# Second gate panel and the output panels of the mixer as seven products in half contractions, with the weight quarters combined in place

## The chip, the cores and the metric

One Trainium2 chip, one of its cores. The metric is device microseconds (us) for one execution of the whole two-layer program. Three timed runs of the kernel before took 1997.31, 1997.37 and 1998.77 us, a median of 1997.37 us. All data are float32.

## The reference

Two decoder layers over 256 tokens of width 2048. A layer is a mixer (one input projection, whose columns go partly to sliding-window attention and partly to a gated delta rule, then one output projection) and a mixture of experts, each followed by a residual add and a LayerNorm.

```python
def hybrid_mixer(h, w_in, sinks, conv_w, a_log, dt_bias, dn_norm_w, w_out, cos, sin):
    proj = h @ w_in                                   # 256 x 2048 times 2048 x 5392
    sq, sk, sv, dn_qkv, dn_z, dn_a, dn_b = jnp.split(proj, cuts, axis=-1)
    ...
    attn_out = sliding_window_attention(sq, sk, sv, sinks)
    ...
    o = gated_delta_rule(dq, dk, dv, g, beta)
    o = (o * lax.rsqrt(jnp.mean(o * o, axis=-1, keepdims=True) + RMS_EPS)
         * dn_norm_w.astype(jnp.float32) * jax.nn.silu(z))
    return jnp.concatenate([attn_out, dn_out], axis=-1) @ w_out      # 2048 x 2048

for l in range(DEPTH):
    mix = hybrid_mixer(x, w_in[l], ...)
    x = layer_norm(ALPHA * x + mix, ln1_g[l], ln1_b[l])
    ffn = grouped_moe(x, router_w, router_bias, w_gate[l], w_up[l], w_down[l])
    x = layer_norm(ALPHA * x + ffn, ln2_g[l], ln2_b[l])
```

The change concerns the columns `dn_z` (the gate, 1024 columns, two panels of 512) of the input projection and the output projection `@ w_out` (2048 columns, four panels of 512).

## The kernel before, in words

**Panels and pieces.** The projections are worked off in panels of 512 output columns. A panel's weights come in four pieces of 512 rows (1 MB each), `j` = 0 to 3, in the order of the table `ORDER`, into a ring of four slots; TensorE frees a slot with `ring_free`, and SyncE issues the next load. Panels 0 to 10 are the input's (0: k and v; 1, 2: q; 3 to 8: delta-rule q, k, v; 9, 10: the gate z), 11 to 14 are the output's. A plain panel (`k_step`, L871; the last one in `last_panel`, L953) multiplies for each of its 16 blocks of 128 rows two token tiles of 128 by 512 columns: 32 matmuls.

**Seven products.** Panels in `FAST` (1, 2, 9, 13) use a Strassen-Winograd scheme: the two token tiles, pairs of row blocks and the two halves of the columns make a 2x2 block product that takes seven products instead of eight (`fast_unit`, L919; 28 units of two 256-column matmuls for a panel). It needs sums of the activations (`add_sums`), differences of the weight quarters (`combine`: four operations of 128x512 for each piece; VectorE for panels 1 and 2, GpSimd, here called POOL, for panels 9 and 13, L619 to L624) and the collection of the products out of four PSUM banks (`copy_first` on ScalarE, `collect` on VectorE, L1809 to L1816). Before, `combine` writes to spare buffers as soon as a piece has landed; only one of its results goes back into the ring.

**The delta rule.** After panel 9 the delta rule runs in two halves of four heads. In each, the 128x128 triangular systems of the chunks are inverted level by level (TensorE L1190, VectorE L2100, L2104, L2109), then the states and outputs follow, and `head_norm` (L2134 to L2140) normalises and gates them. TensorE works in program order; between the steps of the chain the code calls `meanwhile(n)`, which takes the next n matmul steps from a written-out list `left`: before, single k-steps of panels 10, 11 and 12. The last quarters of 11 and 12 come behind the chain, then fast panel 13, then plain panel 14. LayerNorm 1 (`layer_norm`, L2179 to L2186, VectorE) is done for token tile 0 while TensorE does tile 1 of panel 14.

**Experts.** SyncE then streams the weights of 16 experts, two at a time in 24 pieces of 1 MB, of which 16 have a place before the first pair starts (`first_home`, `first_pair`).

## Time and profile before

| | |
|---|---|
| median of three runs | 1997.37 us |
| the profiled execution | 1998.46 us, its span 1996.7 us |
| granted TensorE clock | 0.997 |
| TensorE busy | 1921.4 us (96% of the span) |
| VectorE busy | 686.5 us (34%) |
| ScalarE busy | 329.5 us (17%) |
| GpSimd busy | 103.0 us (5%) |
| HBM traffic | 535.73 MB read, mean 269 GB/s |

In the first layer the mixer takes from 0 to about 508 us, LayerNorm 1 and the router to 533 us, the experts to 985 us; the second layer repeats this. Busy shares are averages over these stages. A mark in brackets behind a row of a timeline says how long the engine sat idle before the row and what ended it. A float32 matmul is two instructions in the trace, so "x4" in a row of TensorE is two matmuls.

### The profile page before, as it was taken

To read this page: it belongs to the slowest core of one execution; us is meant where nothing else is said; L and a number is where in the kernel's file an instruction comes from. 1 tells how busy PE (TensorE), PEld (TensorE's weight loads), DVE (VectorE), ACT (ScalarE), POOL (GpSimd) and SP (SyncE) were. 2 spreads that over 40 slices of the span, in tenths; PEclk is the share of its full clock that TensorE was granted. 3 is DMA by queue.
4 is the path that set the end of the run, shared out by engine and by line. 5 is a ranking of instruction groups with operands and counts; after the bars stand their busy time and mean duration, and the time that the engine had idled before them with its cause. 6 is when DMAs were issued, how large, how long until landed. Compare 5 with 4: busy or idle time off the path is not lost.

```text
span 1996.7 us, 27957 instructions
## 1 busy us (share of the span) xinstructions
PE 1921.4 (96%) x11409; PEld 1194.3 (60%) x11409; DVE 686.5 (34%) x1385; ACT 329.5 (17%) x616; POOL 103.0 (5%) x174
## 2 busy tenths in 40 slices
PE   8999999999999999999899999999999999999996
PEld 7888886666644434444488888766665444443443
DVE  5444434553501111111483434445534011111104
ACT  1104220110311110111211231111103111110112
POOL 4000030012000000000000001200210000000000
PEclk9999999999999999999999999999999999999998
DMA  7433342228699999999934434422397999999995
GB/s 243 148 127 127 127 148 86 85 64 321 271 408 422 422 422 422 422 422 422 406 112 146 139 112 147 135 75 68 103 368 275 411 421 422 422 422 422 422 421 243
DMA packets 128842, 539.16 MB, mean 270 GB/s; under 512 B 15856, under 2 KB 20464, under 8 KB 78320
## 3 DMA queue, kind: packets, MB, share of 16 engines
q1 hardware_dynamic: 128752, 537.86, 69.0%
q8 instruction: 68, 1.11, 0.2%
q14 instruction: 22, 0.18, 0.0%
HBM read 535.73 MB, written 2.10 MB: 269 GB/s over the span
## 4 chain that ended last, share of the span: by engine, by line
PE 68%; DMA 25%; DVE 5%; issue 1%; ACT 0%; SPq 0%; DVEq 0%; ACTq 0%
PE bank L860 17%; DMA ring<-in_w_down_dram 13%; DMA ring<-in_w_up_dram 12%; PE bank L1405 10%; PE bank L871 9%; PE bank L919 8%; PE bank L1453 6%; PE bank L1190 3%; PE bank L953 3%; PE bank L1337 3%; PE bank L787 1%; DMA x_t<-in_w_up_dram 1%; PE bank L1066 1%; PE bank L1349 0%; PE bank L1161 0%
## 5 line engine op out<-in xcount | busy, mean ns | idle before, releaser
L860 PE MATMUL bank<-x_t,ring 128*128 128x256 f32 x1536 | 342.6, 382 | 0.0
L860 PEld LDWEIGHTS bank<-x_t,ring 128*128 128x128 f32 x1536 | 288.4, 190 | 48.8 <-issue 11.2
L2333 DVE TENSOR_TENSOR region_a<-bank,region_a 128x512 f32<-128x512 f32 x16 | 11.1, 692 | 566.3 <-PE bank L1405 566.3
L1405 PE MATMUL bank<-ring,region_a 128*64 128x512 f32 x704 | 159.6, 596 | 13.1 <-DMA ring<-in_w_up_dram 13.1
L1337 PEld LDWEIGHTS bank<-prob_t,x_nat 128*128 128x128 f32 x1024 | 115.5, 192 | 12.0 <-issue 11.4
L871 PE MATMUL bank<-ring,mix_acc 128*128 128x512 f32 x256 | 121.3, 604 | 1.4 <-ACT mix_acc L1663 1.4
L1453 PE MATMUL bank<-ring,region_a 128*64 128x512 f32 x512 | 115.1, 594 | 5.9 <-DMA ring<-in_w_down_dram 5.8
L1337 PE MATMUL bank<-prob_t,x_nat 128*128 128x128 f32 x1024 | 118.6, 277 | 0.0
L1405 PEld LDWEIGHTS bank<-ring,region_a 128*64 128x64 f32 x704 | 51.6, 137 | 109.3 <-issue 107.6
L1453 PE MATMUL bank<-region_b,region_a 128*64 128x512 f32 x384 | 113.3, 596 | 1.7 <-ACT region_a L1710 1.7
L2346 DVE SCALAR_TENSOR_TENSOR y_lo<-bank,slot_gate,y_hi 128x512 fp32r<-128x512 f32 x64 | 48.0, 750 | 193.1 <-ACT y_hi L1722 187.9
L919 PE MATMUL bank<-ring,x_t 128*128 128x256 f32 x416 | 100.7, 380 | 0.0
L1405 PE MATMUL bank<-region_b,prob_t 128*64 128x512 f32 x336 | 98.4, 592 | 0.0
L619 POOL TENSOR_TENSOR ring<-ring 128x512 f32<-128x512 f32 x16 | 20.3, 1271 | 1350.7 <-DMA ring<-in_w_in_dram 1002.2
L1453 PEld LDWEIGHTS bank<-ring,region_a 128*64 128x64 f32 x512 | 38.0, 137 | 80.3 <-issue 80.3
L919 PEld LDWEIGHTS bank<-ring,x_t 128*128 128x128 f32 x416 | 78.2, 190 | 12.7 <-POOL ring L622 1.5
L1405 PE MATMUL bank<-ring,prob_t 128*64 128x512 f32 x288 | 65.0, 595 | 13.2 <-DMA ring<-in_w_up_dram 13.2
L1190 PEld LDWEIGHTS bank<-region_a 64*64 64x64 f32 x1920 | 59.1, 135 | 30.3 <-issue 30.3
L1453 PEld LDWEIGHTS bank<-region_b,region_a 128*64 128x64 f32 x384 | 34.5, 137 | 71.1 <-issue 57.1
L2328 DVE TENSOR_TENSOR mix_acc<-bank,mix_acc 128x512 f32<-128x512 f32 x120 | 73.3, 680 | 7.9 <-PE bank L1351 7.8
L1722 ACT ACTIVATE y_hi<-bank,slot_gate 128x512 fp32r<-128x512 f32 x64 | 44.0, 687 | 190.4 <-PE bank L1453 190.4
L919 PE MATMUL bank<-ring,mix_acc 128*128 128x256 f32 x288 | 69.7, 380 | 0.6 <-DVE ring L1846 0.6
(424 smaller groups left out, 2413.0 us busy)
## 6 DMA issues: line engine op xcount, KB each, us to landing
ring<-in_w_up_dram SPq DMA_DIRECT2D x88, 1024.0 KB, 19.5
ring<-in_w_in_dram SPq DMA_DIRECT2D x80, 1024.0 KB, 5.0
ring<-in_w_down_dram SPq DMA_DIRECT2D x64, 1024.0 KB, 23.4
region_b<-in_w_gate_dram SPq DMA_DIRECT2D x48, 1024.0 KB, 19.6
region_b<-in_w_down_dram SPq DMA_DIRECT2D x48, 1024.0 KB, 20.6
ring<-in_w_gate_dram SPq DMA_DIRECT2D x36, 1024.0 KB, 22.4
ring<-in_w_out_dram SPq DMA_DIRECT2D x32, 1024.0 KB, 5.2
x_t<-in_w_up_dram SPq DMA_DIRECT2D x32, 1024.0 KB, 19.1
```

Source lines behind the costliest of these rows:

```text
L619: pool.tensor_tensor(t1, b12, b11, ALU.subtract).then_inc(combined_ready.sem, 1)
L860: m = pe.matmul(b[c // 2][:, (c % 2) * T:(c % 2 + 1) * T], w[:, kk, c * P:(c + 1) * P], xT[:, k, :], start=(k == 0 and c % 2 == 0), stop=( ...
L871: m = pe.matmul(b[t][:, 0:width], lhs[:, k, t * P:(t + 1) * P], w[:, k if kind == "kv" else kk, 0:width], start=(k == 0), stop=(k == KC - 1))
L919: mm = pe.matmul(o, lhs[:, a, :], rhs[:, a, :], start=(j == a == 0 and name in FIRST_IN_BANK), stop=(j == 3 and a == 1), skip_group_check= ...
L953: m = pe.matmul(bank[PAIR_OF_BANKS[i][t]][:, :], mixT[:, k, t * P:(t + 1) * P], piece(n)[:, kk, :], start=(k == 0), stop=(k == KC - 1))
L1190: m = pe.matmul(out_of(t, h)[rows, :], lhs_of(t, h, rows), rhs_of(t, h, rows), start=True, stop=True)
L1337: m = pe.matmul(bank[GATHER_BANKS[b]][:, j * P:(j + 1) * P], x_nat[:, t, c * P:(c + 1) * P], pick2[:, t, :], start=(t == 0), stop=(t == NT ...
L1405: m = pe.matmul(bank[2 + w][rows, :], xg_half[k // 8][:, k % 8 * P + rows.start:k % 8 * P + rows.stop], weights(n + e)[:, kk * PANEL:(kk + ...
L1453: m = pe.matmul(bank[4 + c][rows, :], hid_t[:, f, rows], weights(n + e)[:, c * PANEL:(c + 1) * PANEL], start=(f == 0), stop=(f == FC - 1))
L1722: act.activation(y_hi[:, c * PANEL:(c + 1) * PANEL], bank[4 + c][:, :], ACT.Copy, scale=slot_gate[:, 0:1]).then_inc(hi_ready.sem, 1)
L2328: tt(a, bank[SCATTER_BANKS[n]][:, :], a, ALU.add).then_inc(scat_added.sem, 1)
L2346: stt(out=y_lo[:, cols], in0=bank[4 + c][:, :], scalar=slot_gate[:, 0:1], in1=y_hi[:, cols], op0=ALU.mult, op1=ALU.subtract).then_inc(y_re ...
```

## The change

The second gate panel (10) and the output panels become products of seven as well. The output panels are cut into half contractions: the front half (rows 0 to 1023, the attention part, pieces `j` = 0, 1) of all four, and the back half (pieces 2, 3) of panels 11, 12 and 13. Each half panel has its own seven products over 14 units, is collected by VectorE and added to the residual `x_nat` (`add_half`). Only the back half of panel 14 stays plain. The order of the pieces follows: front halves of 11 to 14, then back halves.

`combine` now works in place on the ring: each quarter is overwritten once the products that need it as loaded (P1, P2, P3) have run, which the semaphore `raw_done` tells. POOL combines panels 9, 10, the four front halves and the back half of 11; VectorE combines panels 1 and 2, and the back halves of 12 and 13. Units are reordered: the as-loaded products of piece n+1 come ahead of the combined ones of piece n.

In VectorE's program the collections stand at chosen places in the delta rule (`between`, and at the start and end of a half). Panel 8 is done one token side after the other. The early loads of six expert pieces stand together behind the last piece of `w_out`, and two more wait for `spare_free`.

```diff
-    FAST = [1, 2, 9, 13]
+    FAST = [(1, (0, 1, 2, 3)), (2, (0, 1, 2, 3)), (9, (0, 1, 2, 3)), (10, (0, 1, 2, 3))]
+    FAST += [(i, (0, 1)) for i in range(N_IN, N_IN + 4)]
+    FAST += [(i, (2, 3)) for i in range(N_IN, N_IN + 3)]
+    GATE0, GATE1, FRONT, BACK = 2, 3, 4, 8
-    PRODUCTS = [("P1", 0, 0), ("P2", 1, 0), ("P6", 1, 1), ("P5", 2, 0), ("P7", 2, 1), ("P4", 3, 1), ("P3", 3, 0)]
+    AS_LOADED, COMBINED = ("P1", "P2", "P3"), ("P5", "P7", "P6", "P4")
@@ POOL and VectorE, combine(): the same on both @@
-                pool.wait_ge(mix_landed[n % RING].sem, ...)
-                pool.tensor_tensor(t1, b12, b11, ALU.subtract).then_inc(combined_ready.sem, 1)
-                pool.tensor_tensor(t2, b22, t1, ALU.subtract).then_inc(combined_ready.sem, 1)
-                pool.tensor_tensor(b12, b22, b12, ALU.subtract).then_inc(combined_ready.sem, 1)
-                pool.tensor_tensor(t4, b21, t2, ALU.subtract).then_inc(combined_ready.sem, 1)
+                pool.wait_ge(raw_done.sem, raw_done.at(l, 2 * m + 1))
+                pool.tensor_tensor(b11, b12, b11, ALU.subtract).then_inc(combined_ready.sem, 1)
+                pool.wait_ge(combined_ready.sem, combined_ready.at(l, 4 * m + 1))
+                pool.tensor_tensor(b12, b22, b12, ALU.subtract).then_inc(combined_ready.sem, 1)
+                pool.wait_ge(combined_ready.sem, combined_ready.at(l, 4 * m + 2))
+                pool.wait_ge(raw_done.sem, raw_done.at(l, 2 * m + 2))
+                pool.tensor_tensor(b22, b22, b11, ALU.subtract).then_inc(combined_ready.sem, 1)
+                pool.wait_ge(combined_ready.sem, combined_ready.at(l, 4 * m + 3))
+                pool.tensor_tensor(b21, b21, b22, ALU.subtract).then_inc(combined_ready.sem, 1)
...
-                for f in range(2, N_FAST):
-                    for j in range(4):
+                for f in range(GATE0, BACK + 1):
+                    for j in FAST[f][1]:
                         combine(l, f, j)
@@ TensorE @@
+                def units_of(f):
+                    pieces = FAST[f][1]
+                    loaded = [[(f, j, name) for name in AS_LOADED] for j in pieces]
+                    mixed = [[(f, j, name) for name in COMBINED] for j in pieces]
+                    if f == BACK:
+                        return loaded[0] + mixed[0] + loaded[1] + mixed[1]
+                    units = loaded[0]
+                    for n in range(1, len(pieces)):
+                        units = units + loaded[n] + mixed[n - 1]
+                    return units + mixed[-1]
...
-                left = [(10, k, t) for k in range(KC) for t in range(NT)]
-                left += [(i, k, t) for i in (11, 12) for k in range(8) for t in range(NT)]
-                left += [(i, k, t) for i in (11, 12) for k in range(8, 12) for t in range(NT)]
+                left = [unit for f in range(GATE1, BACK) for unit in units_of(f)] + units_of(BACK)[:7]
...
-                fast_panel(13)
+                meanwhile(len(left))
+                fast_panel(BACK, 7)
+                fast_panel(BACK + 1)
+                fast_panel(BACK + 2)
                 last_panel()
@@ VectorE @@
-                combine(0, 3)
+                for j in range(1, 4):
+                    combine(0, j)
...
-                combine(1, 0)
+                def between(half, lev):
+                    if (half, lev) == (0, 2):
+                        dve.wait_ge(pv_read.sem, pv_read.at(l, n_q // 2))
+                        add_sums(mixT, front_sums, 0, 4)
+                    if (half, lev) == (0, 4):
+                        collect_second_sixth(GATE1)
+                        collect_fifth_seventh(GATE1)
+                    if (half, lev) == (0, 5):
+                        collect_third_fourth(GATE1)
+                    if (half, lev) == (1, 1):
+                        collect_third_fourth(FRONT + 1)
+                    if (half, lev) == (1, 2):
+                        add_half(FRONT + 1)
+                    if (half, lev) == (1, 4):
+                        add_sums(mixT, back_sums, 4, 6, 4)
...
                         dve.wait_ge(o1_done.sem, o1_done.at(l, 1))
+                        collect(FRONT)
+                        add_half(FRONT)
...
+                for f in range(BACK, N_FAST):
+                    collect(f)
+                    add_half(f)
+                    if f < N_FAST - 1:
+                        for j in FAST[f + 1][1]:
+                            combine(f + 1, j)
```

How the order changes, at three places. First VectorE at the start of the second layer: the last pieces of panel 1 are combined (`ring<-ring`, four rows a piece), x is rescaled (`x_nat<-x_nat,region_cd`), panel 1 is collected and rotated. Before:

```order
L1889 COPY v_nat<-bank 128x128
L1844 TENSOR_TENSOR ring<-ring 128x512
L1846 TENSOR_TENSOR ring<-ring 128x512
L1847 TENSOR_TENSOR ring<-ring 128x2x256
L1849 TENSOR_TENSOR ring<-ring 128x512
L1899 TENSOR_TENSOR x_nat<-x_nat,region_cd 128x2048 x2
L1902 TENSOR_TENSOR x_nat<-x_nat,region_cd 128x2048 x2
L1844 TENSOR_TENSOR ring<-ring 128x512
L1846 TENSOR_TENSOR ring<-ring 128x512
L1847 TENSOR_TENSOR ring<-ring 128x2x256
L1849 TENSOR_TENSOR ring<-ring 128x512
L1809 TENSOR_TENSOR region_cd<-bank,first_product 128x2x256
```

The same place now, from the last piece of panel 1 on:

```order
L1874 TENSOR_TENSOR ring<-ring 128x2x256
L1876 TENSOR_TENSOR ring<-ring 128x2x256
L1879 TENSOR_TENSOR ring<-ring 128x2x256
L1881 TENSOR_TENSOR ring<-ring 128x2x256
L1930 TENSOR_TENSOR x_nat<-x_nat,region_cd 128x2048 x2
L1933 TENSOR_TENSOR x_nat<-x_nat,region_cd 128x2048 x2
L1816 TENSOR_TENSOR region_cd<-bank,first_product 128x2x256
L1825 TENSOR_TENSOR region_cd<-bank,region_cd 128x2x256
L1826 TENSOR_TENSOR region_cd<-bank,region_cd 128x256
L1833 TENSOR_TENSOR region_cd<-bank,region_cd 128x2x256
L1860 TENSOR_TENSOR v_rot<-region_cd,cos_t 128x512
```

The first piece of panel 2 was combined ahead of panel 1's collection; it now comes behind collection and rotation, and the last piece of panel 1 waits for its own as-loaded products.

Second, VectorE at the start of the second half of the delta rule, from the last two operations of `head_norm` of the first half. Before:

```order
L2138 TENSOR_TENSOR region_cd<-region_cd,rms 128x512
L2140 TENSOR_TENSOR region_cd<-region_cd 128x512
L2055 TENSOR_SCALAR region_a<-bank,gc 128x128 x4
L2065 TENSOR_TENSOR region_a<-bank,region_a 128x512
L2069 TENSOR_TENSOR region_a<-bank,region_a 128x256 x2
```

And now, the same stretch:

```order
L2195 TENSOR_TENSOR region_cd<-region_cd,rms 128x512
L2197 TENSOR_TENSOR region_cd<-region_cd 128x512
L1816 TENSOR_TENSOR ring<-bank,first_product 128x2x256
L1825 TENSOR_TENSOR ring<-bank,ring 128x512
L1826 TENSOR_TENSOR ring<-bank,ring 128x256
L1833 TENSOR_TENSOR ring<-bank,ring 128x512
L1849 SCALAR_TENSOR_TENSOR x_nat<-x_nat,ring 128x2x512
L2104 TENSOR_SCALAR region_a<-bank,gc 128x128 x4
```

Five operations (collection and residual add of the first front half) now stand ahead of the decay's four.

Third, TensorE behind the chain of the second half: L787 (now L793) transposes the gated outputs. Before:

```order
L871 MATMUL bank<-ring,mix_acc 128x512 x2
L787 MATMUL bank<-ident,region_cd 128x128 x4
L871 MATMUL bank<-ring,mix_acc 128x512 x11
L787 MATMUL bank<-ident,region_cd 128x128 x4
L871 MATMUL bank<-ring,mix_acc 128x512 x9
```

And now (the sources of the products are the ring and, in turn, `mix_acc` and its sums in `ring` and `x_t`):

```order
L928 MATMUL bank<-ring,mix_acc 128x256 x2
L928 MATMUL bank<-ring 128x256 x2
L793 MATMUL bank<-ident,region_cd 128x128 x4
L928 MATMUL bank<-ring 128x256 x6
L928 MATMUL bank<-ring,mix_acc 128x256 x2
L928 MATMUL bank<-ring 128x256 x6
L928 MATMUL bank<-ring,mix_acc 128x256 x6
L928 MATMUL bank<-ring,x_t 128x256 x6
L793 MATMUL bank<-ident,region_cd 128x128 x4
L928 MATMUL bank<-ring,x_t 128x256 x2
```

Eleven plain steps between the two transposes became 13 units (26 matmuls of 256 columns).

## Rows read from the trace of the kernel before

**Rows 1.** Busy time by stage (windows); columns as in the first line.
```profile
core 0: us, PE busy (x) PEld busy (x) DVE busy (x) ACT busy (x) POOL busy (x), PEclk, DMA share, GB/s
297.00:508.00 211.00, 209.81 (x1764) 133.55 (x1763) 101.39 (x202) 19.56 (x32) 21.08 (x16) 1.00 0.41 148
...
585.00:640.00 55.00, 55.00 (x288) 24.98 (x286) 8.97 (x15) 9.29 (x16) 0.00 (x0) 1.00 1.01 417
640.00:985.00 345.00, 322.24 (x1630) 144.44 (x1627) 53.27 (x90) 46.04 (x80) 0.00 (x0) 1.00 1.01 421
```

**Rows 2.** The chain that ended last: start us, us, what.
```profile
300.85 4.29 PE bank L871 x10
...
456.64 24.17 PE bank L919 x112
480.81 27.48 PE bank L953 x64
...
510.07 2.35 DVE region_a L2179
```

**Rows 3.** Timeline of VectorE, layer norm of tile 0, start of tile 1.
```profile
494.58 0.69 DVE L2165 SCALAR_TENSOR_TENSOR x_nat<-x_nat,bank 128x512 f32<-128x512 f32 x1 [10.32 <-PE bank L953]
...
498.80 3.92 DVE L2186 SCALAR_TENSOR_TENSOR x_nat<-region_a,ln_s 128x512 f32<-128x512 f32 x4
```

**Rows 4.** Timeline of POOL, combining without and with company.
```profile
437.13 1.26 POOL L622 TENSOR_TENSOR ring<-ring 128x512 f32<-128x512 f32 x1
438.36 1.71 POOL L624 TENSOR_TENSOR ring<-ring 128x512 f32<-128x512 f32 x1
```

**Rows 5.** Timeline of VectorE, a level, the second half's start, its end.
```profile
328.32 0.76 DVE L2104 TENSOR_TENSOR region_a<-bank,region_a 128x256 f32<-128x256 f32 x2 [2.31 <-PE bank L1190]
...
372.93 1.13 DVE L2055 TENSOR_SCALAR region_a<-bank,gc 128x128 f32<-128x128 f32 x4 [2.78 <-PE bank L1161]
...
376.94 0.69 DVE L2071 TENSOR_TENSOR region_a<-bank,region_a 128x512 f32<-128x512 f32 x1
...
393.59 0.42 DVE L2096 TENSOR_TENSOR region_a<-region_a,ident_c 128x256 f32<-128x256 f32 x1
...
436.68 0.69 DVE L2149 TENSOR_TENSOR region_cd<-bank,region_cd 128x512 f32<-128x512 f32 x1
437.40 1.54 DVE L2134 TENSOR_TENSOR region_a<-region_cd 128x512 f32<-128x512 f32 x1
```

**Rows 6.** Timeline of TensorE, where it would wait for those.
```profile
378.06 1.04 PE L787 MATMUL bank<-ident,region_b 128*128 128x128 f32 x8
...
394.56 1.15 PE L1190 MATMUL bank<-region_a 64*64 64x64 f32 x32
...
437.42 0.66 PE L787 MATMUL bank<-ident,region_cd 128*128 128x128 f32 x4
...
448.64 7.99 PE L871 MATMUL bank<-ring,mix_acc 128*128 128x512 f32 x18 [0.69 <-ACT mix_acc L1663]
```

**Rows 7.** Timeline of VectorE, second layer: rescaling of x, panel 1.
```profile
1027.87 4.49 DVE L1899 TENSOR_TENSOR x_nat<-x_nat,region_cd 128x2048 f32<-128x2048 f32 x2
1032.39 4.49 DVE L1902 TENSOR_TENSOR x_nat<-x_nat,region_cd 128x2048 f32<-128x2048 f32 x2
...
1039.46 0.68 DVE L1809 TENSOR_TENSOR region_cd<-bank,first_product 128x512 f32<-128x512 f32 x1
...
1046.52 0.69 DVE L1844 TENSOR_TENSOR ring<-ring 128x512 f32<-128x512 f32 x1 [0.22 <-DVE region_cd L1914]
```

**Rows 8.** Timeline of TensorE, second layer: panel 1, decay inputs, panel 2.
```profile
1012.87 1.89 PE L919 MATMUL bank<-ring,x_t 128*128 128x256 f32 x8
...
1037.57 1.93 PE L984 MATMUL bank<-x_t,prob_t 128*32 128x256 f32 x32
...
1048.08 1.97 PE L919 MATMUL bank<-ring,mix_acc 128*128 128x256 f32 x8 [0.60 <-DVE ring L1846]
```

**Rows 9.** Timeline of VectorE beside POOL's second operation (435.57 to 437.17).
```profile
435.96 0.68 DVE L2147 TENSOR_TENSOR region_cd<-bank,gfac 128x512 f32<-128x512 f32 x1
```

More of the change, by code:

```diff
@@ L175, in trunk @@
         spare = ring[:, RING:RING + 2, :].rearrange("p r n -> p (r n)")
-        def combined(m, which):
-            at = (m % 2) * 6 * HW + which * 2 * HW
-            return spare[:, at:at + 2 * HW].rearrange("p (a n) -> p a n", a=2)
         mix_acc = sb("mix_acc", [P, KC * T])
@@ L877, in k_step @@
-                    if tiles[-1] == 0:
-                        return
-                    if k == KC - 1:
-                        m.then_inc(proj_done.sem, 1)
-                        owed[0] += kind != "kv"
-                    elif kk == 3 and kind != "kv":
-                        m.then_inc(ring_free.sem, 1)
-                def fast_unit(i, j, name):
-                    f = FAST.index(i)
-                    m, n = 4 * f + j, ORDER.index((i, j))
-                    src, added, sums = (xT, 2, x_sums) if i < N_IN else (mixT, 4, mix_sums)
-                    s1, s2, s3, s4 = (v[:, 2 * j:2 * j + 2, :] for v in sums)
-                    t1, t2, t4 = (combined(m, which) for which in range(3))
+                            m = pe.matmul(b[t][:, 0:2 * kv_dim], xT[:, k, t * P:(t + 1) * P], kv_w[:, k, :],
+                                          start=(k == 0), stop=(k == KC - 1))
@@ L913, in fast_unit @@
-                    if name in ("P6", "P5", "P7", "P4"):
-                        seen = {"P6": 2, "P5": 2, "P7": 3, "P4": 4}[name]
-                        pe.wait_ge(combined_ready.sem, combined_ready.at(l, 4 * m + seen))
-                    _, at, half = next(x for x in PRODUCTS if x[0] == name)
-                    o = bank[FAST_BANKS[i][at]][:, half * HW:(half + 1) * HW]
+                        if i >= N_IN and j < 2:
+                            pe.wait_ge(pv_read.sem, pv_read.at(l, n_q // 2))
+                        elif i >= N_IN:
+                            pe.wait_ge(to_read.sem, to_read.at(l, j))
@@ L1101, in _ @@
                     .then_inc(gc_done.sem, 1)
-                panel(8)
+                for side in range(2):
+                    for k in range(KC):
+                        k_step(8, k, (side,))
                 pe.wait_ge(rows_ready.sem, rows_ready.at(l, 1))
@@ L1234, in _ @@
                     meanwhile(1)
-                    assert not left or left[0][0] > 10
                     pe.wait_ge(inv_ready.sem, inv_ready.at(l, (half + 1) * LEVELS))
@@ L1817, in collect, with add_half @@
                     dve.wait_ge(fast_read.sem, fast_read.at(l, 3 * f + 3))
+                def collect(f):
+                    collect_second_sixth(f)
+                    collect_fifth_seventh(f)
+                    collect_third_fourth(f)
+                def add_half(f):
+                    i = FAST[f][0] - N_IN
+                    xs = x_nat[:, :, i * PANEL:(i + 1) * PANEL]
+                    held, at = half_panel(f)
+                    mixed = held[:, at:at + NT * PANEL].rearrange("p (t n) -> p t n", t=NT)
+                    if f < BACK:
+                        s.do(stt(out=xs, in0=xs, scalar=ALPHA, in1=mixed, op0=ALU.mult, op1=ALU.add))
+                    else:
+                        s.do(tt(xs, xs, mixed, ALU.add))
@@ L1917, in _ @@
                     if i == 0:
-                        for j in range(1, 4):
+                        for j in range(4):
                             combine(1, j)
@@ L2101, in _ @@
                         m.then_inc(masked_ready.sem, 1)
+                        between(half, lev)
                         dve.wait_ge(tlt_done.sem, tlt_done.at(l, n_tlt + lev))
@@ L2121, in _ @@
                     m.then_inc(inv_ready.sem, 1)
+                    if half:
+                        collect(FRONT + 2)
+                        add_half(FRONT + 2)
                     if half == 0:
```

351 lines of the change are left out of this document (171 added, 180 removed).

## The prediction, made before the changed kernel was run

> **What bounds the kernel now.** I read the windows by stage first. In the mixer's second part (297 to 508 us) TensorE is busy 209.8 of 211 us at full granted clock, the DMA engines 41% of it, VectorE half of it [rows 1]. Among the experts the picture turns: at 585 to 640 us TensorE is full and the DMA at 417 GB/s, from 640 us to 985 us the DMA runs at 421 GB/s and TensorE idles 23 us. So the experts end a fixed time after they start, whatever the mixer does, provided that the 16 pieces with early homes have landed; what the mixer saves or loses shows in full, once for each of the two layers. The chain of waits agrees: in the mixer it is TensorE's matmuls almost without a break [rows 2], until LayerNorm 1 on VectorE.
>
> **TensorE's own work.** A plain step is 4.29/5 = 0.858 us, a plain panel 27.48 us, a fast panel 24.17 us, so a unit 24.17/28 = 0.863 us [rows 2]. From behind panel 9 to the end of the projections there were three plain panels in steps (3 x 27.46), one fast and one plain: 134.0 us. Now there are 28 + 7 x 14 = 126 units and 16 plain matmuls: 108.8 + 13.7 = 122.5 us. Saved: 11.5 us a layer, 23.0 us in all. Nothing else that TensorE does changes. The rest is what VectorE, POOL and their waits give back.
>
> **Half-hidden work in the delta rule.** TensorE takes one unit between the steps, as before, and works in order. So each late VectorE result stalls it.
> - Level 2 of half 0: `add_sums`, four 512-wide operations of 0.69 us and their gaps, 2.85 us, into an idle stretch of 2.31 us [rows 5]. It delays the inverse by 0.6 us. The pieces of the collections at levels 4, 5, 1 and 2 are 0.7 to 1.9 us and fit there.
> - Start of half 1: collecting (0.69 + 0.69 + 0.42 + 0.69 and gaps, 2.6 us) and `add_half` (1024 wide, 1.3 us) stand ahead of the decay, into 2.78 us of idle time; 1.1 us late. TensorE has 0.43 us to spare there (376.94 + 0.69 = 377.63 against 378.06) [rows 5, 6]. 0.7 us.
> - Start of the inverse, half 1: 0.73 us more against 394.56 - 394.01 = 0.55 us [rows 5, 6]. 0.2 us.
> - Each fast group needs its banks emptied. I went through the units one by one: the second-sixth, fifth-seventh and third-fourth collections stand in VectorE's order before the units that overwrite those banks are reached, so no further wait, 0.
>
> **Combining on POOL, behind the products.** POOL needs four operations of 1.26 us and 0.08 us gaps [rows 4], 5.3 us from the end of P1; the last, P4, is reached five units after P1, 4.3 us. In the delta rule units are spread out and this is hidden. In the back half of panel 11 they are dense and the pieces not interleaved: 1.0 us for each of two pieces, the transposes between give 0.5 us back, 1.5 us. For panels 12 and 13 VectorE combines after it has collected the group before: 0.7 + 1.3 us, then four times 0.72, 4.9 us from the end of the last P4, where TensorE has six as-loaded units, 5.2 us. No wait, by 0.3 us.
>
> **Contention of VectorE and POOL.** VectorE's operations with both inputs in SBUF grow where they meet a POOL operation: 1.54 us instead of 0.69 at 437.40, which ends 0.55 us behind POOL's (437.13 + 1.26), and POOL's next takes 1.71 instead of 1.26 [rows 4, 5]. So a meeting costs VectorE about 0.85 us. Before, POOL worked 21 us in this stretch (16 operations) [rows 1]; now, panel 9 left out, 56 operations, 71 us. Where VectorE's path is the one TensorE waits for:
> - the outputs of half 1: `head_norm` of tile 0 must be over for `o_ready`, which came at 437.37 against TensorE's 437.42 [rows 5, 6]. Two more of its operations now meet POOL: 1.5 us (both ends: 0 to 2.5);
> - masks and inverses at the start of both halves' levels, the decay's mask in half 1: 0.5 + 0.8 + 0.4 us (0 to 4);
> - POOL itself delayed in the back half of 11 by `add_half` and `add_sums`: 0.5 us (0 to 1.5).
> Together 3.7 us a layer; 0 if the phases miss, 8 if all meet.
> The Trainium skill (SBUF — State Buffer, Who interferes with whom) says that such an operation and a GpSimd instruction that reads SBUF exclude each other for a whole instruction, so the loser waits for the rest of the other's. On average that would be half of POOL's 1.26 us, 0.63 us a meeting in place of the row's 0.85, and 2.7 us in place of 3.7.
>
> **LayerNorm 1.** Tile 0 takes from 494.58 to 502.72, 8.1 us [rows 3]. It was hidden behind 13.7 us of tile 1; now tile 1 of the last half panel is 6.9 us. Tile 1's norm starts 1.3 us behind its matmuls. An old wait of 0.69 us before the last quarters [rows 6] goes.
>
> **Head of layer 2.** The last piece of panel 1 is now combined after its P3, 20 units in: 1012.87 + 17.3 = 1030.1, two dependent operations end at 1031.6. The rescaling (9.1 us) thus starts 3.8 us later than at 1027.87 [rows 7, 8], the collection ends its first row at 1041.4, and what took 7.1 us from 1039.46 to 1046.52 brings the first combination of panel 2 to 1047.6 and its result to 1048.3. TensorE has only six as-loaded units behind 1039.5: it is ready at 1044.7 and waits 3.6 us in all, where it waited 0.6 [rows 8]. 3.0 us, once; layer 1 has no rescaling and ends its rotation 3 us ahead of need.
>
> **Loads.** A ring slot is held from P1 to P4, and refilled with 12 us in hand. The eight expert pieces now go out together when TensorE is through with panel 12, some 26 us before the end of the projections instead of 28 to 40. Eleven pieces at 2.5 us (1 MB at 421 GB/s [rows 1]) are 27 us, and the first pair starts 25 us behind the projections' end. Hidden with over 10 us in hand: 0.
>
> **The sum.** A layer: -11.5 + (0.6 + 0.7 + 0.2) + 1.5 + 3.7 + 1.3 - 0.7 = -4.2. Twice that and 3.0 is -5.4 us, from the profiled execution's 1998.46: 1993.1. That execution stands 1.1 us above the median of the runs, so against the median 1992.0.
>
> **Rivals.**
> - *Clean overlap.* Phases miss, POOL and VectorE hardly meet: the 3.7 us go. -12.7 us, 1984.7. For it: rows where VectorE reads a bank while POOL works show no growth (0.68 us at 435.96 inside 435.57 to 437.17 [rows 9]), and most of the chain is of that kind. Against: `o_ready` has 0.05 us to spare.
> - *Everything meets.* Contention of 7 us a layer, or another tight place that I take as covered (VectorE's 0.3 us for panels 12 and 13) opens. +1.3 us or somewhat less, 1995 to 2000: no change. For it: POOL's share rises from 21 to over 70 us in that stretch.
> - *Slower: the level loop itself slows.* If VectorE's operations with one input in a PSUM bank also wait while POOL reads SBUF, each of some six levels a layer beside POOL loses two waits of 0.85 us. The path there has only about 0.2 us to spare, so 10 us a layer: 1993 + 20 - 1, about 2012 with all, 2003 with half. It decides from 2.1 us more a layer than in my sum. Against it stands the single pair of rows [rows 9], seen while POOL ran, and for it only that before no level ever ran beside POOL. The same page of the Trainium skill has it that an operation with at most one SBUF input does not contend; by that this rival is worth nothing.
> - *TensorE isn't shortened.* The units would have to run at 0.95 us instead of 0.863, and the 11.5 us a layer would be gone: 2015. The rate of such units is in the trace [rows 2], so I give it no chance of its own.
>
> **Chances.** Forecast 0.45, 1988 to 1995.5; clean overlap 0.22; everything meets 0.23; slower 0.10. What a measurement tells from no change is 0.2%, 4 us. Below 1993.4 lie most of the first and all of the second: faster 0.56. Same: the rest of the first and the third, 0.33. Slower 0.11. The range is 1983 to 2000, from clean overlap with POOL's waits halved to everything meeting; the forecast's own is 1988 to 1995.5.
>
> **What would show it.** TensorE's busy time falls by 20 us or more, and its idle time in each mixer grows by some 7 us, in the second half of the delta rule and at the back half of panel 11, ended by VectorE and POOL. Operations with two SBUF inputs in `head_norm` have a mean of 1 us or more, the level loop's stay at 0.38 us each. A gap of about 2 us ended by VectorE before the combined products of panel 2, in the second layer alone. LayerNorm of tile 1 starts 1 to 1.5 us late. The experts take as long as before. If the level loop slows, if collections leave TensorE idle at the front halves, or if the first pair waits for a load, the prediction is wrong.

## The result, and the profile after

The changed kernel takes 2003.21 us (median of 17 runs, 1999.87 to 2005.69), the kernel before, timed beside it, 1998.76 us (17 runs, 1997.07 to 2000.66). The ratio is 1.0023, 95% interval 1.0016 to 1.0031: slower by some 4.5 us. Forecast were 1992.0 and a range of 1983 to 2000. The profiled execution has a span of 2001.8 us, 5.1 us longer than before.

The first lines of the page of the changed kernel:

```profile
span 2001.8 us, 28926 instructions
...
PE 1907.0 (95%) x11745; PEld 1257.9 (63%) x11745; DVE 772.1 (39%) x1483; ACT 333.7 (17%) x630; POOL 213.5 (11%) x254
```

The windows by stage, with the columns of [rows 1]:

```profile
297.00:508.00 211.00, 201.99 (x1934) 166.28 (x1933) 141.30 (x252) 21.76 (x39) 76.42 (x56) 0.99 0.38 133
585.00:640.00 55.00, 55.00 (x293) 25.66 (x292) 8.97 (x15) 8.40 (x15) 0.00 (x0) 1.00 1.01 419
640.00:985.00 345.00, 321.57 (x1627) 143.85 (x1627) 51.27 (x87) 45.20 (x78) 0.00 (x0) 1.00 1.01 422
```

The experts are as they were. In the mixer's second part TensorE is busy 7.8 us less than in [rows 1], and the stretch is no shorter: the time turned into waits. These are its waits in that part of layer 1 (waiting line, the line waited for, us in total, times, longest):

```profile
PE bank L1187 <- DVE region_a L2147: 3.8, 2, 2.3
PE bank L793 <- DVE region_cd L2206: 1.5, 1, 1.5
PE bank L793 <- DVE region_a L2120: 1.4, 1, 1.4
PE bank L928 <- POOL ring L628: 1.2, 2, 1.0
PE bank L928 <- POOL ring L633: 0.4, 2, 0.2
PE bank L928 <- POOL ring L631: 0.2, 1, 0.2
PE bank L1228 <- DVE region_a L2170: 0.2, 1, 0.2
```

That is ten waits; before, there were two, of 0.7 and 0.2 us. L1187 is the inverse's product at level 1, L793 the transposes of k (behind L2120) and of the outputs (behind L2206), L928 a product of a fast panel, L1228 the last level of an inverse.

The largest group lies at level 1 of the second half. The timeline of VectorE, POOL and TensorE there (start us, us, engine, line, operation):

```profile
398.00 1.27 POOL L626 TENSOR_TENSOR ring<-ring 128x512 f32<-128x512 f32 x1 [8.93 <-PE bank L928]
398.09 1.45 DVE L2146 TENSOR_TENSOR region_a<-region_a,ident_c 128x256 f32<-128x256 f32 x1
399.35 1.32 POOL L628 TENSOR_TENSOR ring<-ring 128x512 f32<-128x512 f32 x1
399.47 1.48 DVE L2147 TENSOR_TENSOR region_a<-region_a,ident_c 128x256 f32<-128x256 f32 x1
...
401.09 1.74 PE L1187 MATMUL bank<-region_a 64*64 64x64 f32 x32 [2.31 <-DVE region_a L2147]
402.76 2.07 PE L928 MATMUL bank<-ring 128*128 128x256 f32 x4
```

An operation that took 0.42 us [rows 5] takes 1.45 and 1.48. Each of the two ends just behind a POOL operation: 398.09 + 1.45 = 399.54 behind 399.27, 400.95 behind 400.67. These two rows alone could also be read as an operation that runs slower while the two overlap. The mixer rows of nine of the traces decide it: an operation of VectorE with both inputs in SBUF that starts inside a POOL instruction ends 0.27 to 0.29 us behind it when it is 256 wide, whether 0.39 or 1.21 us of POOL's instruction were left, and 1.07 to 1.09 us behind it when it is 1024 wide, with 0.31 to 1.21 us left. So it waits until POOL's instruction is over, and the next one meets the next instruction of POOL's chain. The Trainium skill (SBUF — State Buffer, Who interferes with whom) says that the loser waits for the whole of the other instruction; the trace agrees, with about 1.05 us for each here.

The two last rows show a second thing: 16 small products (x32) take 1.74 us and the two matmuls of a unit (x4) 2.07, where they otherwise take 1.15 and 1.13. The windows say why (columns as above, the third number from the end is the granted clock):

```profile
395.00:401.00 6.00, 3.78 (x44) 3.05 (x42) 5.87 (x11) 0.00 (x0) 2.59 (x2) 1.00 0.58 172
401.00:405.00 4.00, 3.91 (x42) 2.99 (x44) 2.33 (x5) 0.00 (x0) 0.02 (x1) 0.57 0.26 102
405.00:410.00 5.00, 5.00 (x104) 4.11 (x100) 2.33 (x7) 0.39 (x1) 4.44 (x4) 1.00 0.02 5
```

Behind the wait of 2.31 us TensorE's clock was at its lower level (1.2 instead of 2.4 GHz) for most of 4 us, which cost 0.6 + 0.9 = 1.5 us. In layer 2 the same wait of 2.3 us left it at 1.00. The changed kernel's runs differ in this: in 8 of the 17 the mean granted clock was 0.995 or less, with a median of 2004.7 us, in the other nine 0.996 or 0.997, with 2002.4. The profiled execution is one of the latter.

The outputs of the second half, where [rows 5] had 0.05 us to spare:

```profile
439.74 1.67 DVE L2191 TENSOR_TENSOR region_a<-region_cd 128x512 f32<-128x512 f32 x1 [2.89 <-ACT prob_t L1647]
...
442.71 1.62 DVE L2195 TENSOR_TENSOR region_cd<-region_cd,rms 128x512 f32<-128x512 f32 x1
...
444.36 1.64 DVE L2197 TENSOR_TENSOR region_cd<-region_cd 128x512 f32<-128x512 f32 x1
...
447.38 0.66 PE L793 MATMUL bank<-ident,region_cd 128*128 128x128 f32 x4 [1.50 <-DVE region_cd L2206]
```

And the back half of panel 11, where it is POOL that loses, to VectorE's 1024-wide addition, and TensorE waits for POOL:

```profile
456.85 1.39 DVE L1849 SCALAR_TENSOR_TENSOR x_nat<-x_nat,ring 128x1024 f32<-128x1024 f32 x1
457.24 2.13 POOL L628 TENSOR_TENSOR ring<-ring 128x512 f32<-128x512 f32 x1
...
459.42 1.13 PE L928 MATMUL bank<-ring,x_t 128*128 128x256 f32 x4 [1.01 <-POOL ring L628]
```

POOL ends a fixed time behind it as well: 457.24 + 2.13 = 459.37, 1.13 us behind 456.85 + 1.39 = 458.24, and 1.11 to 1.14 us wherever a full-width POOL operation had to wait in these traces. Against that, VectorE's operations with an input in a PSUM bank keep their length: those of the level loop stay at 0.38 us each throughout. The layer norm's second tile starts 1.4 us later (511.49 against 510.07 in [rows 2]), 0.3 us of which it has from the projections. The head of layer 2, the answer to [rows 8]:

```profile
1043.85 1.13 PE L928 MATMUL bank<-ring,x_t 128*128 128x256 f32 x4 [0.96 <-DVE region_cd L1816]
...
1050.93 1.10 PE L928 MATMUL bank<-ring,mix_acc 128*128 128x256 f32 x4 [2.18 <-DVE ring L1874]
```

### The profile page after: what moved, and what is told of

Its sections match the earlier page's. It is cut to its first block, busy times and chain, and to the rows that moved or that the text cites. A ratio compares the mean times of both kernels' runs of the same rounds, so it can differ in the third digit from the quotient of the medians.

```text
span 2001.8 us, 28926 instructions
## 1 busy us (share of the span) xinstructions
PE 1907.0 (95%) x11745; PEld 1257.9 (63%) x11745; DVE 772.1 (39%) x1483; ACT 333.7 (17%) x630; POOL 213.5 (11%) x254
## 4 chain that ended last, share of the span: by engine, by line
PE 63%; DMA 26%; DVE 7%; issue 1%; POOL 1%; ACT 1%; SPq 0%; DVEq 0%; POOLq 0%; ACTq 0%
PE bank L852 17%; PE bank L928 15%; DMA ring<-in_w_down_dram 14%; DMA ring<-in_w_up_dram 11%; PE bank L1400 10%; PE bank L1448 5%; PE bank L1187 3%; PE bank L1332 3%; PE bank L869 1%; PE bank L793 1%; DMA x_t<-in_w_up_dram 1%; PE bank L955 1%; DVE x_nat L2232 1%; PE bank L1068 1%; DVE region_a L2225 0%
## 5 line engine op out<-in xcount | busy, mean ns | idle before, releaser
L626 POOL TENSOR_TENSOR ring<-ring 128x512 f32<-128x512 f32 x36 | 49.0, 1362 | 1213.7 <-PE bank L928 1213.7
L928 PE MATMUL bank<-ring,mix_acc 128*128 128x256 f32 x592 | 150.5, 384 | 3.0 <-DVE ring L1874 2.2
L928 PE MATMUL bank<-ring,x_t 128*128 128x256 f32 x576 | 138.2, 382 | 3.7 <-POOL ring L628 2.3
L1332 PEld LDWEIGHTS bank<-prob_t,x_nat 128*128 128x128 f32 x1024 | 115.5, 192 | 12.0 <-issue 11.4
L928 PEld LDWEIGHTS bank<-ring,x_t 128*128 128x128 f32 x576 | 107.5, 190 | 22.0 <-POOL ring L628 3.9
L928 PEld LDWEIGHTS bank<-ring,mix_acc 128*128 128x128 f32 x592 | 108.8, 190 | 19.8 <-issue 2.8
L1332 PE MATMUL bank<-prob_t,x_nat 128*128 128x128 f32 x1024 | 118.6, 277 | 0.0
L928 PE MATMUL bank<-ring 128*128 128x256 f32 x384 | 98.3, 388 | 0.1
L928 PEld LDWEIGHTS bank<-ring 128*128 128x128 f32 x384 | 70.5, 191 | 13.0 <-issue 3.2
```

Source lines behind the costliest of these rows:

```text
L626: pool.tensor_tensor(b11, b12, b11, ALU.subtract).then_inc(combined_ready.sem, 1)
L928: mm = pe.matmul(o, lhs[:, a, :], rhs[:, a, :], start=(j == pieces[0] and a == 0 and name in FIRST_IN_BANK), stop=(j == pieces[-1] and a = ...
L1332: m = pe.matmul(bank[GATHER_BANKS[b]][:, j * P:(j + 1) * P], x_nat[:, t, c * P:(c + 1) * P], pick2[:, t, :], start=(t == 0), stop=(t == NT ...
```

## The experiments

Two theories on the 4.5 us. **A: contention.** VectorE's operations with two inputs in SBUF and POOL's shut each other out for whole instructions, at the places TensorE waits for. **B: added work.** VectorE's own new work (collections, additions, sums) comes late there. Times of different groups of runs are compared through the kernel before, timed beside each group (1998.58, 1998.31 and 1999.21 us); against it the changed kernel stands at +4.5 us.

**POOL's work shrunk.**

```
                 b11, b12, b21, b22 = (quarter(n, row, col) for row in range(2) for col in range(2))
+                if f >= GATE0:
+                    b11, b12, b21, b22 = (b[:, :, 0:8] for b in (b11, b12, b21, b22))
                 pool.wait_ge(raw_done.sem, raw_done.at(l, 2 * m + 1))
```

> GpSimd's four subtractions of a piece work on 8 of each row's 256 columns, for the second gate panels and the output panels alike; all waits stay. This leaves out most of the combining. Theory (VectorE and GpSimd block each other where VectorE has two inputs in SBUF, and GpSimd's own chain is late in the back half of panel 11): the losses read from the trace go, per layer 1.5 us at level 1 of half 0, 0.9 of the 1.6 at the second gates' pair masks of half 1, 2.2 of 2.4 at level 1 of half 1, 1.5 at o_ready, 2 to 2.9 at the back half of panel 11, and 1.5 once where TensorE's clock fell to 0.54 to 0.60 for 4 us in layer 1. That is 17 to 19 us off 2003.2: 1984 to 1987, and L2146, L2147, L2191, L2195 back at 0.42 and 0.69 us. Rival (it is VectorE's own added work, collections and additions, that comes late): -4 us or less, 1999 or more.

Measured 1982.91 us, ratio 0.9919 (0.9906 to 0.9932): -15.7 against before, 20.1 us less than the changed kernel. That is 1 us below what was expected. TensorE's waits in the mixer's second part are of 0.4 us at most, with all of VectorE's added work in place. A stands, B is worth at most 1 us a layer, the sum of these waits. It also shows what the seven products save when nobody gets in their way. It can't tell a meeting from POOL's own time for its chain, since both are gone.

**The same for the back half of panel 11 alone** (`if f == BACK:`).

> The same reduction (8 of 256 columns) for GpSimd's two pieces of the back half of panel 11 alone; this leaves out most of their combining. Theory: only the waits for the chain of four dependent subtractions go, and VectorE's addition beside it is back at its own length: 2 to 2.9 us a layer, -4 to -6 us, 1997.5 to 1999.5. Rival (TensorE is held there by the last outputs' copy and only the releaser's name changes): 0 to -1 us.

Measured 1997.05 us (12 runs, 1992.73 to 2002.22), ratio 0.9990 (0.9982 to 0.9999): 6.0 us less than the changed kernel, by medians, with a wide spread. The projections of layer 1 end at 505.19 us instead of 508.41. The waits for L628, L631 and L633 are gone, all others there. So POOL's chain costs some 3 us a layer in this place, a little over the upper end of what was expected; the rival fell. How much of it is the chain's own length and how much the meeting isn't separated; the longest wait, 1.01 us, stands behind the POOL operation that took 2.13 us instead of 1.27. The spread goes with the granted clock: the three runs above 1999 us have 0.993 or 0.994, the others 0.995 to 0.998.

**Intermediates in PSUM.** Nothing is left out, POOL works as in the changed kernel; the masking of the inverse's first level and the product with q are written back into the bank they came from, so that the next operation has one input in SBUF instead of two.

```
-                        s.link(tt(decay[:, t], decay[:, t], bc(tri[:, :], 1, HALF), ALU.mult))
-                        tt(a_t[:, t], qk, decay[:, t], ALU.mult).then_inc(pair_read.sem, 1)
+                        s.link(tt(qk, qk, decay[:, t], ALU.mult))
+                        tt(a_t[:, t], qk, bc(tri[:, :], 1, HALF), ALU.mult).then_inc(pair_read.sem, 1)
...
-                        s.do(tt(masked[:, t], in_bank(bank[4 + 2 * t]), bc(level_mask[:, 0, :], 1, HALF), ALU.mult))
+                        lt = in_bank(bank[4 + 2 * t])
+                        s.do(tt(lt, lt, bc(level_mask[:, 0, :], 1, HALF), ALU.mult))
...
-                    s.do(tt(inv_c[:, 0], masked[:, 0], bc(ident_c[:, :], 1, HALF), ALU.add))
+                    s.do(tt(inv_c[:, 0], in_bank(bank[4]), bc(ident_c[:, :], 1, HALF), ALU.add))
```

> VectorE's operations with two SBUF inputs at the inverse's first level and at the decay's mask put their intermediate into the PSUM bank it came from, so that each has one SBUF input; nothing is left out, no operation more or less, GpSimd's work as in the changed kernel. Theory: inv_c's pair back from 1.14 to 1.48 us to 0.4 each, TensorE's waits before level 1 fall from 1.45 and 2.31 us to under 0.5, the clock stays at 1.0 behind them in layer 1 of the model: 1.5 + 1.5 to 2.0 + 0.5 a layer and 1.5 once, so -8 to -9.5 us, some of it met again at o_ready: 1994 to 1997. Rival (GpSimd blocks VectorE in any access to SBUF, one input or two): no change, 2003.

Measured 1993.50 us, ratio 0.9974 (0.9966 to 0.9983): 9.5 us less than the changed kernel, just past the expected range, and faster than the kernel before. The rows of 398 to 402 us above now read:

```profile
395.35 1.27 POOL L626 TENSOR_TENSOR ring<-ring 128x512 f32<-128x512 f32 x1 [8.47 <-PE bank L928]
395.45 0.42 DVE L2147 TENSOR_TENSOR region_a<-bank,ident_c 128x256 f32<-128x256 f32 x1
395.79 0.41 DVE L2148 TENSOR_TENSOR region_a<-bank,ident_c 128x256 f32<-128x256 f32 x1
...
396.36 1.15 PE L1187 MATMUL bank<-region_a 64*64 64x64 f32 x32 [0.22 <-DVE region_a L2148]
```

and the window behind it:

```profile
401.00:405.00 4.00, 4.00 (x81) 3.18 (x82) 3.31 (x7) 0.38 (x1) 2.87 (x3) 1.00 0.00 0
```

The same additions run inside the same POOL instruction in 0.42 us. What decides is the number of inputs in SBUF, not that POOL is at work. The waits at o_ready (1.5 us) and for POOL's chain are as before, and that for L2120 has 0.7 of its 1.4 us left. With POOL's work shrunk it is 0.4 us: this rest is VectorE's added collection and addition ahead of the decay, the part of B that is true.

**The head of layer 2.**

```
                 for i in range(2):
                     collect(i)
+                    if i == 0:
+                        combine(1, 0)
                     for t in range(NT):
```

(and `range(1, 4)` in the loop of combinations behind the rotation)

> After collecting panel 1, VectorE combines the first piece of panel 2 before it rotates panel 1's queries, not behind it; nothing is left out. Theory (the head of layer 2 costs 3.2 us because the rescaling, 9 us, starts later and the collection, 2.6, and the rotation, 4.3, stand before that combination): the combination is 4.3 us earlier, TensorE's wait in layer 2 falls by 3 us or a little less, layer 1 is unchanged: 2000 to 2001. Rival (the piece itself arrives late or the wait is for the banks): no change.

Measured 2001.62 us, ratio 1.0010 (1.0001 to 1.0018): 1.4 us less than the changed kernel. In the trace the wait of 2.18 us is gone and nothing takes its place; that of 0.96 us, for the first collection, stays. The edit reaches only what stands behind the rotation; the 3 us expected would have needed an earlier rescaling as well. That the time fell by less than the wait is within the spread of the runs, and in this trace the clock fell behind level 1 of the second half in both layers, in that of the changed kernel in one.

**Is it the wait that brings the clock down?** Two kernels made from the kernel before, in which VectorE repeats one masking ahead of level 1, six times in half 1, or four times in each half:

```
                     s.sync()
+                    for _ in range((0, 6)[half]):
+                        s.link(tt(masked[:, 1], in_bank(bank[6]), bc(level_mask[:, 0, :], 1, HALF), ALU.mult))
                     s.do(tt(inv_c[:, 0], masked[:, 0], bc(ident_c[:, :], 1, HALF), ALU.add))
```

> The kernel before, with six repeats of one 256-wide masking (same operands, same result) on VectorE ahead of level 1 in half 1 of each layer. They cost VectorE about 2.8 us, TensorE had 0.55 us to spare there, so it should stand still for 2.25 us once a layer. Theory (a stretch of idling of about 2.3 us can take TensorE's granted clock to 0.5 for some 4 us, as at 401 to 405 us of the changed kernel, and this costs 1.5 us more on its work): 4.5 us of waits and 1.5 us for each layer where the clock falls, 2004.5 to 2006.5 against 1998.6, with stretches at 0.5 behind the wait. Rival (the fall of the clock there has another cause and only came at the same time): +4.5 us, 2003, clock 1.0 throughout.

> The kernel before, with four such repeats ahead of level 1 in each half of each layer: two waits of about 1.3 us in place of one of 2.25. Theory (only the longer stretch brings the clock down): 2.6 us a layer, +5.2, 2003.8, clock 1.0 throughout: no more than the kernel with one gap although TensorE idles longer. Rival (the fall goes by the idle time in sum, or has nothing to do with it): as much clock lost as with one gap, or none in both, so that this one is slower by 0.7 us.

One gap: 2004.98 us, ratio 1.0032 (1.0020 to 1.0045). Two gaps: 2002.66 us, ratio 1.0021 (1.0012 to 1.0030). The wait in the first, on TensorE's timeline, and the window behind it:

```profile
395.79 1.86 PE L1190 MATMUL bank<-region_a 64*64 64x64 f32 x32 [2.27 <-DVE region_a L2098]
```

```profile
396.00:399.00 3.00, 3.00 (x34) 1.96 (x30) 0.76 (x2) 0.00 (x0) 0.00 (x0) 0.50 0.08 30
```

The two waits of the second kernel, and the window behind the longer one:

```profile
324.34 1.15 PE L1190 MATMUL bank<-region_a 64*64 64x64 f32 x32 [0.81 <-DVE region_a L2098]
...
396.27 1.15 PE L1190 MATMUL bank<-region_a 64*64 64x64 f32 x32 [1.36 <-DVE region_a L2098]
```

```profile
398.00:402.00 4.00, 4.00 (x86) 2.77 (x86) 1.65 (x5) 0.00 (x0) 0.00 (x0) 1.00 0.01 4
```

Behind a wait that POOL had no part in, of 2.27 us, the clock was at 0.50 in layer 1; in layer 2 the same wait left it at 1.00. In the second kernel TensorE waits 0.81 + 1.36 = 2.17 us a layer, nearly as much, and its clock stays at 1.00 through both layers. That a wait of this length can bring the clock down is shown; that it does so every time is not so. In the traces 13 waits of 2.2 to 2.3 us stand in the two mixers, and the clock fell behind eight: behind one of three in the changed kernel, three of three with the back half of panel 11 shrunk, two of two in the head-of-layer experiment, one of two here. The Trainium skill (TensorE: Matmul & The Clock Gate, Part 1: The HAM clock gate) says that the chip watches TensorE's activity in windows that run on regardless of the kernel; that would make the fall a matter of where the wait lies in them, and no run here shows it. The difference of the two times, 2.3 us, has the right sign. The intervals of the two ratios overlap, but the two kernels were timed beside each other, and all six runs with one gap (2004.37 us and more) lie above ten of the eleven with two (2003.38 and less), at a granted clock of 0.996 against 0.997 or 0.998. The one fall in the mixer explains 1.6 us of it (1.86 us for 16 small products instead of 1.15, 2.00 for the plain step behind them instead of 1.13). One more fall, at 1555 us among the experts of the one-gap kernel, followed waits of 0.27 and 0.96 us, and the trace with the back half of panel 11 shrunk has one at the same place; I have no explanation for it.

**Products in another order in the back half of panel 11**, beside the PSUM intermediates:

```
-                left = [unit for f in range(GATE1, BACK) for unit in units_of(f)] + units_of(BACK)[:7]
+                left = [unit for f in range(GATE1, BACK) for unit in units_of(f)]
+                left[-4:-4] = [(BACK, 2, "P1")]
+                left += [(BACK, 2, "P2"), (BACK, 2, "P3"), (BACK, 2, "P5"), (BACK, 3, "P1")]
+                left += [(BACK, 2, "P7"), (BACK, 2, "P6"), (BACK, 2, "P4"), (BACK, 3, "P2")]
```

> The PSUM intermediates of e3_psum_mid, and beside them the order of the products in the back half of panel 11: the first product of its first piece goes ahead of the last four products of the panel half before it, the first product of its second piece ahead of the first piece's last three, so that GpSimd can start on each piece earlier. Nothing left out. Theory (these waits, 1.6 us a layer in the trace, are for GpSimd's chain of four, 5.3 us from the end of the first product): all of them go, -3 us against 1993.5: 1990 to 1991. Rival (the longest of them, 1.0 us, is the meeting of GpSimd's second operation with VectorE's 1024-wide addition, which an earlier start moves but doesn't avoid): -1 us, 1992.5.

Measured 1991.88 us, ratio 0.9965 (0.9951 to 0.9979): -6.4 against before where the PSUM intermediates alone had -5.1, a difference within what the runs can tell, and nearer to the rival's 1992.5 than to the 1990 to 1991 expected. Of five waits for POOL one of 0.2 us is left, but a new one of 1.3 us has come, for the last of the sums (L1796): `add_sums` follows the last transposes, and two of its operations now meet POOL, 1.49 and 1.37 us instead of 0.41 and 0.42.

**All of it**, and the norm of tile 0 from bank 5:

```
-                        s.link(tt(sq, o[:, t], o[:, t], ALU.mult))
+                        held = bank[5][:, :].rearrange("p (h c) -> p h c", h=HALF) if t == 0 else o[:, t]
+                        s.link(tt(sq, held, o[:, t], ALU.mult))
...
-                        s.link(tt(o[:, t], o[:, t], bc(rms[:, 2], 2, P), ALU.mult))
+                        s.link(tt(held, held, bc(rms[:, 2], 2, P), ALU.mult))
...
-                        tt(o[:, t], o[:, t], zz, ALU.mult).then_inc(dn_out.sem, 1)
+                        tt(o[:, t], held, zz, ALU.mult).then_inc(dn_out.sem, 1)
```

> e7_back_first and e4_head_first together, and the norm of tile 0 of the outputs reads and writes PSUM bank 5, which still holds them, so that none of its three 512-wide operations has two SBUF inputs. Nothing left out. Theory: L2191, L2195 and L2197 back from 1.6 to 0.69 us for tile 0, the wait at o_ready (1.5 us a layer) goes, and the head of layer 2 gives 1.6 us as in e4_head_first: -3 and -1.6 against e7_back_first, 1985 to 1987. Rival (the wait at o_ready follows the state's chain on ScalarE, whatever VectorE's lengths): -1.6 us, 1989.

Measured 1984.35 us, ratio 0.9930 (0.9916 to 0.9943). Tile 0's three operations, with POOL at work beside them:

```profile
431.93 0.69 DVE L2199 TENSOR_TENSOR region_a<-bank,region_cd 128x512 f32<-128x512 f32 x1 [2.88 <-ACT prob_t L1651]
...
433.92 0.70 DVE L2203 TENSOR_TENSOR bank<-bank,rms 128x512 f32<-128x512 f32 x1
434.65 0.69 DVE L2205 TENSOR_TENSOR region_cd<-bank,region_cd 128x512 f32<-128x512 f32 x1
...
439.62 1.73 DVE L2203 TENSOR_TENSOR region_cd<-region_cd,rms 128x512 f32<-128x512 f32 x1
```

The last row is the same line for tile 1, which was left with both inputs in SBUF: 1.73 us. The wait at o_ready is down from 1.5 to 0.2 us, that for the transposes of k from 0.7 to 0.4, and the mixer's second part is 2.2 us shorter than in the experiment before.

**Six products instead of four kept behind the last transposes** (`meanwhile(len(left) - 6)`):

> e8_all, with six products of the back half of panel 11 kept behind the last outputs' transposes in place of four. Nothing left out. Theory (the 1.3 us a layer that e7_back_first and e8_all wait for the sums, L1796, come from transposes that are done late while their input has been ready for 8 us; two products more behind them, 1.7 us, cover the sums): -2.5 us against e8_all's 1984.4, 1982. Rival (earlier sums meet the same GpSimd operations, and the wait moves with them): no change, 1984.

Measured 1983.49 us, ratio 0.9925 (0.9911 to 0.9938), the fastest here, 15.7 us below the kernel before and as fast as with POOL's work shrunk. Of the 1.3 us for the sums 0.9 are left, so in the trace the rival was nearer: the sums still meet POOL. Against the kernel ahead of it (-14.0 us) the gain is within what these runs can tell.

**The PSUM intermediates and the norm from bank 5 in the kernel before:**

> The kernel before, with the PSUM intermediates of e3_psum_mid and e8_all at the decay's mask, at the inverse's first level and in the norm of tile 0. Nothing left out. Theory (these edits only give back what meeting GpSimd's operations costs, and before the change it hardly met them): TensorE's waits before, 0.2 us at most at each of these places, stay: 1998 to 1998.6, no change. Rival (operations on PSUM are quicker in themselves, and the gain of e3_psum_mid has little to do with the change): -3 us or more.

Measured 1999.08 us against 1999.21, ratio 0.9999 (0.9990 to 1.0008): nothing. These edits are no gain in themselves; they give back what the change had cost.

## Why the prediction was wrong

The sum was -5.4 us on the profiled execution and came out at +5.1 on its span. By its terms:

**TensorE's own work: right.** -11.5 us a layer. The windows from the first spread of the gates to the end of the projections, for the kernel before, the changed one in both layers, and the one with POOL's work shrunk:

```profile
297.71:508.11 210.40, 209.21 (x1761) 133.20 (x1761) 101.07 (x201) 19.56 (x32) 21.08 (x16) 1.00 0.41 149
```

```profile
298.06:508.41 210.35, 201.34 (x1929) 165.75 (x1929) 141.06 (x252) 21.76 (x39) 76.42 (x56) 0.99 0.38 132
1289.97:1498.77 208.80, 199.81 (x1930) 164.71 (x1930) 141.05 (x252) 21.77 (x39) 76.41 (x56) 1.00 0.38 133
```

```profile
297.57:496.54 198.97, 197.65 (x1929) 165.12 (x1929) 129.24 (x252) 21.99 (x39) 15.69 (x56) 1.00 0.39 139
```

With the waits taken away TensorE is busy 209.21 - 197.65 = 11.6 us less. In layer 1 of the changed kernel it is busy 201.34 us: 1.5 us more than in layer 2, for the clock, and some 2 us more again that go with its waits. What these 2 us are no run shows; the waits put into the kernel before in the two experiments on the clock left its busy time as it was where the clock stayed up (209.16 to 209.24 us). The idle time rose from 1.2 to 9.0 us. Together that is 11.5 us, and the stretch is 0.05 us shorter than before. So the sign I had named, 20 us or more less busy time in the whole program, didn't come: it is 1907.0 us against 1921.4.

**Contention: the step that failed.** I took 3.7 us a layer, 1.5 at o_ready, 1.7 for masks and inverses, 0.5 for POOL itself. The place at o_ready was right: the wait is 1.5 us, and taking it away with the norm from bank 5 gave back 2.2 us, 0.3 of it at another wait. At the masks and inverses the PSUM experiment made the stretch 204.42 us in both layers instead of 210.35 and 208.80: 5.9 us in layer 1, 1.5 of it clock, and 4.4 in layer 2, against the 1.7 I had taken. For all that POOL's work does in the stretch, meetings and chain, I had 3.7 + 1.5 = 5.2 us a layer; without it the stretch of layer 2 falls from 208.80 to 198.97, 9.8 us (4.4 + 2.2 + 3.2 in the separate experiments). Twice the missing 4.6 us and 1.5 us for the clock are 10.7, and the sum was 10.5 us too low; the other terms' errors nearly cancel. Two faults. I priced a meeting at 0.85 us and let each place have part of one; but POOL works in chains of four with gaps of 0.08 us, and VectorE's operations there come in dependent pairs, so when the first is caught the second is caught too: 0.72 + 1.06 us in half 0, 1.03 + 1.06 in half 1. And I gave the phases an even chance, while the schedule ties them together: P1 of a piece, which starts POOL, is one of the units that TensorE takes while VectorE prepares the first level. The same meeting takes place in both layers at the same spot (2.3 us in each).

**The clock: missing.** No term stood for it. In the trace of before the clock is at 1.00 through the mixer's second part [rows 1], and the longest wait there is 0.69 us [rows 6], and I didn't ask what a longer wait would do. 1.5 us, once in the profiled execution, where the stretches of the two layers differ by about that (210.35 against 208.80 us).

**Half-hidden work: small, as predicted.** `add_sums` at level 2 was put at 0.6 and cost 0.2 us. The collection and addition ahead of the decay were put at 0.7 us, and 0.4 is what is left when the contention is out. The collection at the start of the inverse, 0.2: 0.2 is left.

**Back half of panel 11: too low.** Predicted 1.5 + 0.5 - 0.7 = 1.3 us net, 2.0 gross; its removal gave back 3.2 us in layer 1.

**Layer norm 1.3, measured 1.1; head of layer 2 3.0, measured 3.4.** From the projections' end to the experts' gather of x (L1332) it takes 19.3 us instead of 18.2, in every kernel with the change. Panel 3 of layer 2 starts 5.7 us later, of which 2.3 came out of layer 1; TensorE waits there in two places, 0.96 and 2.18 us. That no load is late and that the 0.3 us for panels 12 and 13 hold was right. The last pair of layer 1's experts starts 2.3 us late where the gather had started 1.4 us late. These 0.9 us have no cause in the change that I could find, and the same distance differs from trace to trace, 423.6 to 425.3 us, whichever the kernel (424.3 before, 425.2 after).

**The rivals.** "Everything meets" is what happened; it was priced as if meetings came singly, at 7 us a layer with the end at 2000. With the 9.8 us measured in place of 5.2, and 1.5 for the clock, my own sum would have been 1993.1 + 9.2 + 1.5 = 2003.8 for the profiled execution, which took 2003.48. "The level loop slows" fell: its operations keep 0.38 us each beside POOL, as [rows 9] and the Trainium skill's rule (SBUF — State Buffer, Who interferes with whom) had it, and that the result lies near its 2003 is a coincidence. "Clean overlap" (1984.7) is what the last experiments reached, at 1983.5, by taking the second SBUF input away and changing the order at two places, not by luck of the phases.

## What to carry to other kernels

Before giving an idle engine a chain of SBUF operations, look for each operation with two SBUF inputs on VectorE's path to the busiest engine, and count it as caught, in pairs if it comes in pairs, unless the schedule keeps the two apart. An intermediate that is written back into the PSUM bank it came from takes the operation behind it out of the contention, here at no cost. And where the busiest engine has been without a break, a wait of 2 us may cost more than its length, since the clock can fall behind it.

## What the runs showed of the hardware

- Two-SBUF-input operations of VectorE beside POOL operations of 1.27 us, in the changed kernel: 0.42 became 1.14 to 1.48 us, 0.69 became 1.46 to 1.67. POOL's own beside VectorE's of 0.69 and 1.22 us: 1.27 became 1.60 to 2.13. With one input in a PSUM bank VectorE's took 0.41 to 0.42 us (44 operations of 256 columns in nine traces) and 0.68 to 0.70 (249 of 512) beside the same POOL operations.
- The loser of a meeting ends a fixed time behind the winner, however long it had to wait: VectorE's by 0.27 to 0.29 us (256 columns), 0.54 to 0.56 (512) and 1.07 to 1.09 (1024), POOL's of 512 columns by 1.11 to 1.14 us.
- Writing an operation's result to a PSUM bank instead of SBUF cost VectorE nothing that the rows show: 0.75 us for two of 256 columns either way, 0.70 against 0.69 us for 512.
- TensorE's clock was granted at 0.5 for 3 to 4 us behind eight of 13 waits of 2.2 to 2.3 us in seven traces, and behind none of the four of 0.8 and 1.4 us in the kernel with two gaps. One fall cost 1.5 to 1.6 us of the mixer's second part.
